# Attention of four mixer layers: the copies of the turned shares on ScalarE, and another order of TensorE's small steps

## The reference, cut to what matters

```python
def causal_block_attention(q, k, v, scale, cum=None):
    S = q.shape[1]
    for i in range(S // Q_BLOCK):                    # Q_BLOCK = 128, so two blocks
        lo, hi = i * Q_BLOCK, (i + 1) * Q_BLOCK
        s = jnp.einsum('bqhd,bkhd->bhqk', q[:, lo:hi], k[:, :hi]) * scale
        ...
        p = jax.nn.softmax(jnp.where(mask, s, -jnp.inf), axis=-1)
        outs.append(jnp.einsum('bhqk,bkhd->bqhd', p, v[:, :hi]))
...
    return o.reshape(B, S, d) @ w_out
```

## Time and profile before

| | |
|---|---|
| median of 3 runs | 2819.86 us (2815.72 to 2822.91) |
| the profiled execution, its own time | 2819.86 us |
| its span, first to last instruction | 2818.1 us |
| mean granted clock of TensorE | 0.978 of full speed |
| busy: PE, PEld, DVE, ACT, POOL | 95%, 81%, 36%, 49%, 70% of the span |
| dsa0, from 948 us | 154 us |
| fox, from 1468 us | 138 us |
| mla, from 1972 us | 136 us |
| dsa1, from 2474 us | 154 us |

### The profile page before, as it was taken

The page is one execution under the profiler, slowest core; times in us unless marked ns, Lnnn a source line. Parts: engine busy times, 40 slices in busy tenths (PEclk is TensorE's granted clock), DMA queues, the critical chain, the costliest instruction groups (busy, mean ns, idle before and its releaser), DMA issues.

```text
span 2818.1 us, 35997 instructions
## 1 busy us (share of the span) xinstructions
PE 2682.6 (95%) x15016; PEld 2287.8 (81%) x15016; DVE 1004.0 (36%) x1695; ACT 1385.0 (49%) x1667; POOL 1970.8 (70%) x432
## 2 busy tenths in 40 slices
PE   7879988799999999999999999999989999999998
PEld 4768986589888877888889888888868888877887
DVE  6666559443311254112123311212441121145212
ACT  3544453354554564445456444545534454455543
POOL 3557754277688765887877588787628878865785
PEclk8999989899999999999999999999989999999999
DMA  8577755255455543555545255555416555543553
GB/s 325 189 263 268 267 198 187 98 202 187 158 220 194 182 148 134 200 190 195 194 164 195 105 216 188 195 193 179 165 45 224 191 184 197 190 179 120 179 185 114
DMA packets 80390, 521.77 MB, mean 185 GB/s; under 512 B 8908, under 2 KB 9292, under 8 KB 24420
## 3 DMA queue, kind: packets, MB, share of 16 engines
q1 hardware_dynamic: 80228, 519.47, 51.0%
HBM read 518.38 MB, written 1.05 MB: 184 GB/s over the span
## 4 chain that ended last, share of the span: by engine, by line
PE 82%; DVE 9%; ACT 5%; DMA 2%; issue 1%; POOL 1%; SPq 0%; DVEq 0%; ACTq 0%
PE acc L554 15%; PE acc L515 14%; PE mb L492 10%; PE cb L492 10%; PE cb L467 9%; PE mb L494 5%; PE cb L494 5%; ACT whi L1131 2%; PE mb L607 2%; DVE AR L1825 2%; PE acc L819 1%; PE acc L467 1%; DMA raw<-in_w 1%; DMA AR<-in_a 1%; DVE hT L1775 1%
## 5 line engine op out<-in xcount | busy, mean ns | idle before, releaser
L2397 POOL TENSOR_TENSOR wlo<-raw,whi 128x2048 fp32r<-128x2048 f32 x428 | 1970.6, 4614 | 823.7 <-ACT whi L1131 736.7
L1131 ACT ACTIVATE whi<-raw 128x2048 fp32r<-128x2048 f32 x428 | 818.4, 1914 | 628.2 <-PE cb L492 245.5
L515 PE MATMUL acc<-whi,ARR 128*128 128x512 f32 x1312 | 367.0, 392 | 2.7 <-DVE ARR L1775 2.7
L492 PE MATMUL cb<-hT,whi 128*128 128x512 f32 x1280 | 335.4, 393 | 1.5 <-ACT AR L1235 1.5
L492 PE MATMUL mb<-hT,whi 128*128 128x512 f32 x1280 | 334.1, 393 | 0.4 <-DVE ARR L1775 0.3
L467 PE MATMUL cb<-hT,whi 128*128 128x256 f32 x1536 | 283.4, 287 | 7.9 <-DVE cb L1840 7.9
L515 PEld LDWEIGHTS acc<-whi,ARR 128*128 128x128 f32 x1312 | 246.1, 188 | 55.1 <-issue 4.8
L554 PE MATMUL acc<-whi,hT 128*128 128x512 f32 (+2 forms) x928 | 262.0, 391 | 7.0 <-DVE hT L1775 5.7
L492 PEld LDWEIGHTS mb<-hT,whi 128*128 128x128 f32 x1280 | 230.2, 189 | 43.7 <-issue 2.8
L492 PEld LDWEIGHTS cb<-hT,whi 128*128 128x128 f32 x1280 | 229.6, 189 | 42.3 <-issue 1.9
L467 PEld LDWEIGHTS cb<-hT,whi 128*128 128x128 f32 x1536 | 241.1, 193 | 16.6 <-issue 16.1
(11 more groups left out here) (319 smaller groups left out, 3416.0 us busy)
## 6 DMA issues: line engine op xcount, KB each, us to landing
raw<-in_w SPq DMA_DIRECT2D x436, 1024.0 KB, 4.8
AR<-in_a SPq DMA_DIRECT2D x80, 512.0 KB, 5.6
gb<-in_lng SPq DMA_DIRECT2D x12, 512.0 KB, 5.7
gb<-in_lnb SPq DMA_DIRECT2D x12, 512.0 KB, 6.5
gb<-in_normg SPq DMA_DIRECT2D x8, 512.0 KB, 7.7
x<-in_x SPq DMA_DIRECT2D x1, 1024.0 KB, 8.4
out<-x SPq DMA_DIRECT2D x2, 512.0 KB, 2.7
cn<-in_cn SPq DMA_DIRECT2D x1, 560.0 KB, 6.5
```

The lines of the kernel that those rows point to most:

```text
L492: ins = pe.matmul(to[j], wh[:, w], hT[:, k, :], start=k == 0, stop=k == 7)
L515: ins = pe.matmul(acc[:, 2 * t + c, 0:c1 - c0], xs[y], a[:, kk * width + c0:kk * width + c1], start=first and kk == 0 and m == 0, stop=las ...
L1131: ac.activation(whi[i % NH][:, :], raw[u % NR][:, :], ACT.Copy).then_inc(*up(s_hi, ("hi", i)))
L2397: po.tensor_tensor(wlo[i % NH][:, :], raw[(i + NADA) % NR][:, :], whi[i % NH][:, :].bitcast(F32), ALU.subtract).then_inc(*up(s_lo, ("lo", i)))
```

## The change

- The copy of a turned share (item 5) goes from VectorE's program to ScalarE's, in all four mixers. In ScalarE's queue it stands in the odd step, where that step had nothing.
- dsa0 and dsa1: W(0) to W(3) go from the generator beside the value products to the head of the first list of `tail`. The second 48 value matmuls give a slot at every fifth instead of every fourth.
- mla: `started` is 5 instead of 9. No step stands in the loop of the keys any more; S(0) to S(4) stand in the loop of the values, each ahead of a product instead of behind it. S(5) to S(10) and W(0) to W(7) alternate in the first list of `tail`. ScalarE's `unit(h + 5)` comes before the first exponentials, `values_out(0)` behind S(2), and `unit(h + 6)` and `unit(h + 7)` behind S(3) and `values_out(1)`. VectorE copies all keys before the first mask.

```diff
-        started = {"dsa0": 11, "dsa1": 11, "fox": 18, "mla": 9}
-        weighed_early = {"dsa0": (0, 1, 2, 3), "dsa1": (0, 1, 2, 3), "fox": (), "mla": ()}
+        started = {"dsa0": 11, "dsa1": 11, "fox": 18, "mla": 5}
...
             if name == "mla":
-                return (W(0, 1, 2, 3) + S(9) + W(4, 5, 6, 7) + T(0, 0) + T(0, 1),
-                        S(10) + S(11) + W(8, 9) + S(12) + S(13) + W(10, 11) + S(14) + T(1, 0) + S(15) + W(12, 13) + S(17)
-                        + W(14, 15) + T(1, 1))
-            return (S(11) + W(4, 5, 6, 7) + T(0, 0) + T(0, 1),
+                return (S(5) + W(0, 1) + S(6) + W(2, 3) + S(7) + T(0, 0) + S(8) + W(4, 5) + S(9) + W(6, 7) + S(10) + T(0, 1),
+                        S(11) + W(8, 9) + S(12) + S(13) + W(10, 11) + S(14) + T(1, 0) + S(15) + W(12, 13) + S(17) + W(14, 15)
+                        + T(1, 1))
+            return (W(0, 1, 2, 3) + S(11) + W(4, 5, 6, 7) + T(0, 0) + T(0, 1),
...
@@ TensorE, dsa @@
-                    for i in weighed_early[name]:
-                        weigh(name, i)
-                        yield
-                rows_units(hi2, *hk, ready, (name, "v"), last=True, beside=beside, every=4)
+                rows_units(hi2, *hk, ready, (name, "v"), last=True, beside=beside, every=5)
@@ TensorE, mla: loop of the keys, then loop of the values @@
-                    for s in ((), (0, 1), (2,), (3, 4))[g]:
-                        step(name, s, "cb", score_ready)
...
+                        for s in ((0, 1), (2,), (3,), (4,))[2 * t + c]:
+                            step(name, s, "cb", score_ready)
                         to = claim(("acc", 2 * t + c), ("mv", t, c))
...
-                        for s in ((5, 6), (7,), (8,), ())[2 * t + c]:
-                            step(name, s, "cb", score_ready)
@@ ScalarE @@
+            def turned_share(name, i):
+                ...
+                copy(PT[name][i % m][:, 0:w], view(key)[:, 0:w], (name, "turned", i), ("free", key))
             def step(name, s):
-                for i in steps(name)[s][0]:
+                scores, turns = steps(name)[s]
+                for i in scores:
                     exps(name, i)
+                for p in turns:
+                    turned_share(name, p)
@@ ScalarE, mla @@
+                unit(h + 5)
                 step(name, 0)
-                unit(h + 5)
-                for s in range(1, 5):
-                    step(name, s)
+                step(name, 1)
+                step(name, 2)
+                values_out(0)
+                step(name, 3)
                 unit(h + 6)
-                for s in range(5, 8):
-                    step(name, s)
-                values_out(0)
-                step(name, 8)
+                step(name, 4)
+                values_out(1)
                 unit(h + 7)
-                values_out(1)
                 finish(name)
@@ VectorE @@
-            def turned_share(name, i):
-                ...
-                dv.tensor_copy(PT[name][i % m][:, 0:w], view(key)[:, 0:w]).then_inc(
-                    *up(s_dv, (name, "turned", i), ("free", key)))
             def step(name, s):
-                scores, turns = steps(name)[s]
-                for i in scores:
+                for i in steps(name)[s][0]:
                     biased(name, i)
-                for p in turns:
-                    turned_share(name, p)
```

More of the change, by code:

```diff
@@ L1033, in turn_queries @@
                     ins.then_inc(*up(s_mm, ("full", ("mqrT", t))))
[L1035 to L1040, removed]
                 rot = unit()
@@ L1070, in mla, with score_ready @@
                         turn_queries(1)
-                    for s in ((), (0, 1), (2,), (3, 4))[g]:
-                        step(name, s, "cb", score_ready)
+                def score_ready(s):
+                    t, h0 = order[name][s]
+                    q.wait_ge(*on("mqn", h0 // 8, t))
+                    q.wait_ge(*on("mkn", h0 // 4))
+                    q.wait_ge(*on("mqrT", t))
+                    q.wait_ge(*on("mkrT"))
                 h, wh, wl = unit()
@@ L1419, in exps @@
                         *up(s_ac, *([(name, "exp", i)] if j else [])))
+            def turned_share(name, i):
+                key = (name, "p", i)
+                m = len(PT[name])
+                w = 256 * (order[name][i][0] + 1)
+                q.wait_ge(*on("full", key))
+                if i >= m:
+                    q.wait_ge(*on(name, "weighed", i - m))
+                copy(PT[name][i % m][:, 0:w], view(key)[:, 0:w], (name, "turned", i), ("free", key))
             def step(name, s):
-                for i in steps(name)[s][0]:
+                scores, turns = steps(name)[s]
+                for i in scores:
                     exps(name, i)
+                for p in turns:
+                    turned_share(name, p)
             def finish(name):
@@ L2154, in result @@
                                  ALU.mult).then_inc(*up(s_dv, (name, "osum", t, g), ("free", key)))
[L2156 to L2159, removed]
             def finish(name):
@@ L2166, in finish @@
                     elif what == "weigh":
-                        weighed(name, at[0])
+                        if pv_last(name, at[0]):
+                            t, h0 = order[name][at[0]]
+                            result(name, t, h0 // 8)
                     else:
@@ L2257, in dsa @@
                     step(name, s)
-                for i in weighed_early[name]:
-                    weighed(name, i)
                 finish(name)
@@ L2339, in mla @@
                 queries_out(1)
-                keys_out(1)
-                step(name, 0)
-                keys_out(2)
-                step(name, 2)
-                keys_out(3)
-                for s in range(3, started[name]):
+                for g in range(1, 4):
+                    keys_out(g)
+                for s in range(started[name]):
                     step(name, s)
```

## The result

The changed kernel takes 2846.21 us (median of 4, 2845.54 to 2846.84), the one before 2820.82 beside it: ratio 1.0093, 95% interval 1.0076 to 1.011. It is slower, 3 us from the 2843 forecast. Its profiled execution took 2840.79 us, span 2839.0, clock 0.970.

A forecast was written before the change was run, and what follows sets the result against it. TensorE, busy 2682.6 of 2818.1 us, was taken to set the end. mla 13, dsa stalls 2 x 2.5, dsa clock 2 x 2.5 and fox 0.5 gave +23.5 us, so 2843 us (chance 0.55), range 2835 to 2849.

The forecast's parts named there:

- The two terms: dsa0 and dsa1, each: +2.5 us of waiting up to the first output matmul, and 2.5 us lost to half clock.
- The stated bounds: dsa0 and dsa1: the loss to half clock in each stage was put between 0 and 4.7 us.
- fox: fox at S(14): copies of tiles 10 and 11 stand behind later exponentials; +0.5 us, bounds 0 and 1.
- mla, the stalls: mla at full clock: 10.7 us of new stalls, less 1.1 for covered waits, +9.6 where the clock stays.
- The queue sum: All stages: adding up, step by step, what stands ahead of each copy; put as good to some 0.3 us.
- the sign that the prediction named: mla in the profile after: gaps of about 3 and 4 us between 2040 and 2060, clock below 0.85.
- mla, the clock: mla: 9.5 us at half clock behind each of four gaps; idle +6.4, work +6.3 us; taken as +13.
- full clock throughout: mla: the stage would end at -2 us if the clock never fell, "which nothing speaks for".
- (a): Rival, stalls without further loss of clock: mla +6.5, dsa +5, fox +0.5, about +12, 2832 us; chance 0.2.
- (c): Rival, the clock does not come back between gaps: mla +16, each dsa +7.2, +31, 2851 us; chance 0.08.
- (b): Rival, faster: ScalarE serves mla's copies earlier than VectorE did, removing a gap and half clock; 2811 us; chance 0.07.
- (d): Rival: stalls fall into misjudged slack and mla's better spacing of early steps pays for them; 2820 us; chance 0.1.

The follow-up runs named there:

- fill_all: The changed kernel with dummy matmuls ahead of its large stalls in mla, dsa0 and dsa1: 2822.42 us, ratio 1.0016 to the kernel before.
- engine_alone: The kernel before, in its old order, with only the 64 copies moved from VectorE to ScalarE: 2828.64 us, ratio 1.0027 to the kernel before.
- order_alone: The changed kernel with its new order but the copies left on VectorE: 2828.09 us, ratio 1.0034 to the kernel before.
- after_again: The changed kernel itself, run and profiled once more: 2841.9 us, ratio 1.0084 to the kernel before.
- engine_queue: engine_alone with ScalarE's late mla queue reordered to fit the copies, and VectorE's low part of T(1,0) moved ahead: 2806.53 us, ratio 0.9951 to the kernel before.
- all_queues: engine_queue with ScalarE's queue in dsa0 and dsa1 also reordered, copies ahead of the last high part and values: 2804.68 us, ratio 0.9955 to the kernel before.
- mla_queue: The changed kernel with ScalarE's queue reordered in dsa0, dsa1 and mla, and VectorE's in mla: 2814.66 us, ratio 0.9986 to the kernel before.

## Why the prediction was right

**The bound.** TensorE stayed the engine that sets the end, and each gap and each slower matmul showed in the time.

**dsa.** ScalarE's order was as written: high part, values, then copies 8 and 9, which end by 1060.2 (1059.8 and 1060.4 forecast). The gap is 2.19 us (2.7), the first output matmul at 1062.36 (1062.0). The two terms come apart in fill_all: +2.4 us at full clock (2.5 forecast), and the clock's 2.4 and 1.9 (2.5). The stated bounds, 0 and 4.7, were far wider than needed.

**fox** +0.3 (0.5 forecast); engine_alone has the same, order_alone nothing, so it comes with the copies on ScalarE. In the profile after, TensorE waits 0.26 us for a copy at 1558.26, where the trace of before has no gap.

**mla, the stalls.** At full clock they can be read from fill_all, from the first dummy to the step behind: W(6) 2051.14 - 2048.15 = 3.0 us (3.1 forecast), S(11)'s second turn 2059.94 - 2056.01 = 3.9 (3.9). In the same way W(2) has 1.3 (1.6), T(0,0) 0.7 (1.0), W(10) 2.6 (2.5), S(15) 3.4 (3.2). The queue sum held at each place to 0.3 us. In the profile after they are shorter, 1.47 at W(6) and 2.41 at the turn, because TensorE at half clock gets there later. So the sign that the prediction named, gaps of about 3 and 4 us, did not show in the profile, though the sum behind it was right; the clock was to be below 0.85 and is 0.85.

**mla, the clock.** The stage came out at +12.9 for the 13 forecast, but two errors cancel in it. TensorE's idle time grew by 3.9 us (148.79 - 136.30 less the 8.6 of before), not 6.4, and its work by 9.0, not 6.3. The step that was off is the length at half clock: 9.5 us behind each gap, 38 in all. The windows have about 45 us in this execution and 53 in after_again, since a gap that falls into a stretch at half clock prolongs it. The figure for full clock throughout, -2, "which nothing speaks for", was measured with the gaps filled: -1.3. In part they must cancel, as TensorE at half clock comes later to the same waits; that they do so to 0.1 us is luck, and after_again has +14.8 for the same kernel.

**The sum.** 23.5 forecast against 22.3 in the stages and 20.9 in the span, since the rest of this execution was 1.4 us shorter. The medians differ by 25.4. after_again has 24.6 in its stages, so some 2 us of the difference lie in how long the clock stays down in one execution. The rest is open: the changed kernel's other four executions there took 2845.5 to 2846.8 us, and no trace of them was kept. What makes the clock come back earlier in one execution than in the other stays open too.

**The rivals.** (a) fell: it had the stalls without slower matmuls, and of the 22.3 us 14.2 are slower matmuls. fill_all's +3.8 is no test of its 12, since it also takes away the half clock that the kernel before has in mla. (c) was the nearest: after_again's mla, +14.8 of its +16, though the dsa stages lost no more than the forecast gave them. (b) was wrong for this queue, but its mechanism exists. Its condition was copy 8 ending less than 3.4 us after S(10). In engine_queue S(10) begins at 2047.57 and takes 2.5 us, and the copy ends at 2051.9, 1.8 us behind it. The 5 us of engine time in its bracket count all 64 copies at the 512-wide form's 0.08 us, though half of them are 256 wide; VectorE lost 31.1 us and ScalarE gained 24.8. (d) fell too: TensorE's idle time in mla grew from 8.6 to 12.5 us, and at full clock the stalls cost 10.8 against fitted queues (134.60 against 123.75). fill_all's mla is 1.3 us under the one of before, but at a clock of 1.00 against 0.92, so that doesn't show that the spacing of the early steps pays.

## What to carry to other kernels

When work moves to another engine, its duration there is the smaller part. Write out what stands ahead of it in that engine's queue when its consumer arrives: here the same 64 copies on ScalarE went with a loss of 7 us (engine_alone) or a gain of 14 (all_queues), by the order of the queues. Among small tiles a gap can cost several times its length (1.84 us of gaps cost 8.1 more in mla_queue) or nothing beyond it, so look at the granted clock before and behind each. Dummy matmuls in a gap are a cheap test of how much of a loss is the clock; but they take away all that a kernel loses to the clock, so set it beside another at full clock, not beside one that loses to the clock too. The lasting remedy is the order of the queue that the gap waits for.

## What the hardware showed beyond that

The same gap doesn't always do the same. In engine_alone a gap of 1.23 us at 2057.28 left the clock at full speed, where those of 2.39 and 2.45 us brought it down; in mla_queue 1.17 and 0.67 us, 2.2 us apart, were followed by 19 us at half clock (2040 to 2059). Nor does it take the same time to come back: in the changed kernel it did so at 2070, 3 us behind a gap of 2.41 us, in one execution, and in the other it stayed down past that gap until 2094.
